# Third layer norm of a three-layer kernel: four PSUM places for rows, another order of statistics, roots and additions

## What is computed

```python
def layer_norm_2(x, g, b):
    xf = x.astype(jnp.float32)
    mu = jnp.mean(xf, axis=-1, keepdims=True)
    var = jnp.mean(jnp.square(xf - mu), axis=-1, keepdims=True)
    y = (xf - mu) * lax.rsqrt(var + LN_EPS)
    return (y * g.astype(jnp.float32) + b.astype(jnp.float32)).astype(x.dtype)
...
    h = layer_norm_2(DEEPNORM_ALPHA * h + gate[:, None, :] * y, ln_g[i], ln_b[i])   # last layer: h is the output
```

## Time and profile before

| what | before |
|---|---|
| median of 3 runs | 2042.57 us |
| the profiled execution | 2042.94 us |
| its span in the profile | 2041.1 us |
| TensorE busy | 1982.5 us (97%) |
| DVE busy | 1082.7 us (53%) |
| ACT busy | 830.3 us (41%) |
| POOL busy | 817.8 us (40%) |
| last matmul of the output projection ends | about 2017.2 us |
| last DVE instruction ends | about 2038.5 us |

### The profile page before, as it was taken

The page is one execution under the profiler, slowest core; times in us unless marked ns, Lnnn a source line. Parts: engine busy times, 40 slices in busy tenths (PEclk is TensorE's granted clock), DMA queues, the critical chain, the costliest instruction groups (busy, mean ns, idle before and its releaser), DMA issues.

```text
span 2041.1 us, 36967 instructions
## 1 busy us (share of the span) xinstructions
PE 1982.5 (97%) x14892; PEld 1641.6 (80%) x14892; DVE 1082.7 (53%) x2243; ACT 830.3 (41%) x1641; POOL 817.8 (40%) x610
## 2 busy tenths in 40 slices
PE   7999999999999999999999999999999999999896
PEld 6888888888887788888888788778888888888784
DVE  5566556766855665556666733734434334334626
ACT  4110110110126565566667610744554554555501
POOL 3433333333346622212122435645435435435546
PEclk9999999999999999999999999999999999999998
DMA  4332332332222301011001323221111111112243
GB/s 159 134 103 83 104 103 73 114 103 73 93 93 83 136 22 35 35 35 35 22 25 35 134 96 112 78 92 43 47 55 45 45 56 45 46 53 64 94 134 119
DMA packets 51063, 156.02 MB, mean 76 GB/s; under 512 B 5584, under 2 KB 9296, under 8 KB 50768
## 3 DMA queue, kind: packets, MB, share of 16 engines
q1 hardware_dynamic: 49888, 152.40, 22.5%
q10 hardware_dynamic: 1008, 1.27, 0.2%
HBM read 132.94 MB, written 20.71 MB: 75 GB/s over the span
## 4 chain that ended last, share of the span: by engine, by line
PE 64%; DVE 3%; POOL 2%; issue 2%; ACT 2%; DMA 1%; DVEq 0%; SPq 0%; POOLq 0%; ACTq 0%
PE psum L902 16%; PE psum L903 14%; PE psum L904 14%; PE psum L1086 8%; PE psum L1037 7%; PE psum L1053 5%; PE psum L911 1%; POOL w_lo L721 1%; ACT logits L1365 1%; DMA w_raw<-weights_in 1%; DVE logits L1782 1%; POOL rstd L744 0%; PE psum L1064 0%; POOL out_tile L884 0%; DVE u_lo L1669 0%
## 5 line engine op out<-in xcount | busy, mean ns | idle before, releaser
L902 PE MATMUL psum<-u_hi,w_hi 128*128 128x512 f32 (+1 forms) x1440 | 544.2, 378 | 2.6 <-DVE u_lo L1669 2.6
L903 PE MATMUL psum<-u_lo,w_hi 128*128 128x512 f32 (+1 forms) x1440 | 524.9, 364 | 0.0
L904 PE MATMUL psum<-u_hi,w_lo 128*128 128x512 f32 (+1 forms) x1440 | 524.7, 364 | 0.0
L719 POOL CAST w_hi<-w_raw 128x1024 fp32r<-128x1024 f32 x140 | 156.7, 1119 | 835.6 <-DMA w_raw<-weights_in 835.5
L721 POOL TENSOR_TENSOR w_lo<-w_raw,w_hi 128x1024 fp32r<-128x1024 f32 x140 | 350.2, 2501 | 11.2
L902 PEld LDWEIGHTS psum<-u_hi,w_hi 128*128 128x128 f32 x1440 | 271.8, 189 | 55.3 <-DVE u_lo L1669 4.4
L904 PEld LDWEIGHTS psum<-u_hi,w_lo 128*128 128x128 f32 x1440 | 272.0, 189 | 45.0
L903 PEld LDWEIGHTS psum<-u_lo,w_hi 128*128 128x128 f32 x1440 | 272.4, 189 | 38.4
L1365 ACT ACTIVATE logits<-logits,neg_max 128x640 f32<-128x640 f32 (+2 forms) x288 | 226.1, 785 | 70.9 <-DVE neg_max L1782 69.3
L1388 ACT ACTIVATE prob_t<-psum 128x320 f32<-128x320 f32 (+1 forms) x288 | 118.8, 413 | 245.2 <-PE psum L1053 244.9
L1374 ACT ACTIVATE logits<-logits,row_rec 128x640 f32<-128x640 f32 (+1 forms) x288 | 218.1, 771 | 0.0
(11 more groups left out here) (165 smaller groups left out, 2999.4 us busy)
## 6 DMA issues: line engine op xcount, KB each, us to landing
w_raw<-weights_in SPq DMA_DIRECT2D x140, 512.0 KB, 3.6
w_ada<-w_ada_in SPq DMA_DIRECT2D x48, 512.0 KB, 3.5
residual<-act_buf SPq DMA_DIRECT2D x4, 2048.0 KB, 7.6
tab<-bias_tab_in SPq DMA_DIRECT2D x16, 496.5 KB
res<-residual SPq DMA_DIRECT2D x26, 256.0 KB, 3.4
y_all<-staged SPq DMA_DIRECT2D x24, 256.0 KB, 4.9
act_buf<-x_t_in SPq DMA_DIRECT2D x8, 512.0 KB, 13.5
staged<-a_y SPq DMA_DIRECT2D x6, 640.0 KB, 2.9
```

What stands on the lines that cost most here:

```text
L719: pool.tensor_copy(w_hi[:, slot, :], w_raw[:, slot, :]).then_inc(w_hi_done, 1)
L902: pe.matmul(out, wh, xh, start=first, stop=False)
L903: pe.matmul(out, wh, xl, start=False, stop=False)
L904: return pe.matmul(out, wl, xh, start=False, stop=last)
```

## The change

Four things. (1) The norms' row places become 4 (banks 0 to 7), of which the third norm's tiles 5 and 6 use the third and fourth; tile 4 has the place of tile 2, tile 7 that of tile 3. So tile 4 waits for ACT's reading of tile 2, tile 7 for that of tile 3, and tiles 5 and 6 wait for none. The two earlier norms keep places n modulo 2. (2) The small per-tile buffers get four places, which moves every buffer behind them by 96 bytes. (3) DVE's order at the end becomes: statistics 4, product 3, statistics 5, scales 4, statistics 6, scales 5, product 4, statistics 7, scales 6, product 5, scales 7, product 6, product 7. (4) POOL's order becomes: root 2, addition 1, root 3, addition 2, root 4, addition 3, roots 5 and 6, addition 4, root 7, additions 5 and 6. ACT's and SyncE's order stay, and no arithmetic changes.

```diff
+LAST_SLOTS = {4: (0, 2), 5: (2, None), 6: (3, None), 7: (1, 3)}
+
+
+def row_slot(n):
+    return LAST_SLOTS.get(n - LN0[2], (n % ROW_SLOTS, None))[0]
+
+
+def slot_before(n):
+    if n - LN0[2] in LAST_SLOTS:
+        i = LAST_SLOTS[n - LN0[2]][1]
+        return None if i is None else LN0[2] + i
+    return n - ROW_SLOTS if n >= ROW_SLOTS else None
...
-    stats = sb("stats", [P, ROW_SLOTS, 12])
-    mean_var = sb("mean_var", [P, ROW_SLOTS, 2])
+    stats = sb("stats", [P, ROW_SLOTS + 2, 12])
+    mean_var = sb("mean_var", [P, ROW_SLOTS + 2, 2])
...
-    ps_rows = [bank(2 * n, 2) for n in range(ROW_SLOTS)]
+    ps_rows = [bank(2 * n, 2) for n in range(ROW_SLOTS + 2)]
...
-            s = slice(n % ROW_SLOTS, n % ROW_SLOTS + 1)
+            s, before = slice(row_slot(n), row_slot(n) + 1), slot_before(n)
             pool.wait_ge(ln_var, n + 1)
-            if n >= ROW_SLOTS:
-                pool.wait_ge(ln_norm, n - ROW_SLOTS + 1)
+            if before is not None:
+                pool.wait_ge(ln_norm, before + 1)
...
-        for t in range(1, S // P - 1):
+        for t in range(1, 4):
             root(2, t + 1)
             add_row(t)
+        root(2, 5)
+        root(2, 6)
+        add_row(4)
+        root(2, 7)
+        add_row(5)
+        add_row(6)
...
-            if n >= ROW_SLOTS:
-                pe.wait_ge(ln_norm, n - ROW_SLOTS + 1)
-            turn_tiles(ps_rows[n % ROW_SLOTS], [act_buf[:, k, t * P:(t + 1) * P] for k in range(KT)]).then_inc(ln_turned, 1)
+            if slot_before(n) is not None:
+                pe.wait_ge(ln_norm, slot_before(n) + 1)
+            turn_tiles(ps_rows[row_slot(n)], [act_buf[:, k, t * P:(t + 1) * P] for k in range(KT)]).then_inc(ln_turned, 1)
...
         normalise_last(3)
+        statistics(LN0[2] + 5)
         scales(LN0[2] + 4)
-        for i in range(4, S // P):
-            if i + 1 < S // P:
-                statistics(LN0[2] + i + 1)
-            normalise_last(i)
-            if i + 1 < S // P:
-                scales(LN0[2] + i + 1)
+        statistics(LN0[2] + 6)
+        scales(LN0[2] + 5)
+        normalise_last(4)
+        statistics(LN0[2] + 7)
+        scales(LN0[2] + 6)
+        normalise_last(5)
+        scales(LN0[2] + 7)
+        normalise_last(6)
+        normalise_last(7)
```

More of the change, by code:

```diff
@@ L321, in build @@
     corr = sb("corr", [P, GROUPS, PAD])
-    stats = sb("stats", [P, ROW_SLOTS, 12])
-    mean_var = sb("mean_var", [P, ROW_SLOTS, 2])
-    neg_mean = sb("neg_mean", [P, ROW_SLOTS])
-    rstd = sb("rstd", [P, ROW_SLOTS])
-    var_eps = sb("var_eps", [P, ROW_SLOTS])
+    stats = sb("stats", [P, ROW_SLOTS + 2, 12])
+    mean_var = sb("mean_var", [P, ROW_SLOTS + 2, 2])
+    neg_mean = sb("neg_mean", [P, ROW_SLOTS + 2])
+    rstd = sb("rstd", [P, ROW_SLOTS + 2])
+    var_eps = sb("var_eps", [P, ROW_SLOTS + 2])
     minus_half = sb("minus_half", [P, 1])
@@ L1478, in normalise_last @@
         def normalise_last(i):
-            place = (LN0[2] + i) % ROW_SLOTS
+            place = row_slot(LN0[2] + i)
             act.wait_ge(ln_scaled, KT + i + 1)
@@ L1636, in statistics @@
         def statistics(n):
-            s, rows = n % ROW_SLOTS, ps_rows[n % ROW_SLOTS]
+            s, rows = row_slot(n), ps_rows[row_slot(n)]
             dve.wait_ge(ln_turned, n + 1)
@@ L1645, in scales @@
         def scales(n):
-            s = n % ROW_SLOTS
+            s = row_slot(n)
             dve.wait_ge(ln_rstd, n + 1)
```

## The result

The changed kernel took 2073.5 us (median of 4 runs, 2070.96 to 2078.62), the kernel before 2043.2 beside it: a ratio of 1.015, interval 1.0138 to 1.0162. It is 1.5% slower, where +0.45 us was forecast.

A forecast was written before the change was run, and what follows sets the result against it. TensorE is busy 97% of 2041.1 us, so only the last 23 us count, bound by DVE and POOL excluding each other. +0.9, 0, -0.4, +0.6, -0.65 make +0.45 on 2042.57: 2043.0 us, range 2041.2 to 2045.2.

The forecast's parts named there:

- rival C: Large buffers moved by 96 bytes slow the first inputs' transfers at the start: 0 to 0.5 us, up to 2043.5; chance 0.10.
- 0.03 for slower: Chance given to a time more than 4.1 us slower, from a layout cost far over its bound or something unseen.
- The sign that the prediction gave for C: TensorE's last product would end more than 0.5 us later than before.
- Transposes in one go: End of kernel: tiles 4 to 7 transposed together from 2018.18, 0.72 us each; worth nothing by itself.
- Addition 4 later by 0.9: POOL at the end: addition 4 starts at 2026.85 against 2025.97, behind moved statistics, root 6 and product 4.
- Root 6 and product 4 at once, either order: Both come up within 0.1 us and run one after the other, both over at 2026.8 to 2026.9.
- Additions 4 and 5 unchanged: POOL at the end: step between these additions stays 1.08 + 0.38 + 2.35, still 3.8 us apart.
- The half step ahead of addition 6: First half of DVE's product 7 runs before POOL's addition 6, adding 0.6 us there; three half steps remain afterwards.
- rival B: DVE keeps POOL out through product 6 and tile 7's half steps, addition 6 comes last: +1.2 to +2.0 us; chance 0.10.
- The sum: End of kernel: +0.9, 0, -0.4, +0.6 and -0.65 give +0.45 us, bounds 0.0 to +0.6.
- Rival A: Roots were the delay at the end; moving them frees POOL to run beside products: 4.7 us earlier, 2037.9 us; chance 0.05.
- the shared resource: At the end, DVE's product and POOL's work exclude each other for whole instructions: 3.81 to 3.84 us a tile.

The follow-up runs named there:

- run 9: The whole change with mean_var, neg_mean and rstd laid ahead of the split weights, so weights and large buffers both move by 96 bytes, against the kernel before: 2042.8 us, ratio 1.0000.

## Why the prediction was wrong

**The failed step is rival C, the layout.** I had seen that every large buffer moves by 96 bytes, but asked only whether DVE minds (0.83 and 0.81 us on two neighbours) and how far the first transfers could suffer (0.5 us). From one engine's row I wrote that "engines don't mind". I had no row on TensorE, the one engine that is busy for 97% of the span, and such a row couldn't be had for its large products: in the kernel before all split weights and all streams stand at one distance modulo 256, so its trace is silent on any other. The rule that a condition which the trace doesn't show is bounded from both sides was needed here most: with 5952 large matmuls, 1 ns each is 6.0 us, more than the 4.1 that can be told from no change. An unbounded cost per matmul should have widened the range upwards and taken more than 0.03 for slower. The term was set at 0 to 0.5 us and measured 28 to 30. The sign that the prediction gave for C came: TensorE's last large product ended at 2045.39 + 0.40 = 2045.79 us, 28.6 later than before, where 0.5 was the bound. What the extra time is made of wasn't foreseen in any of the rivals, for C priced DVE and the transfers: here it is 6.6 ns more from one large matmul to the next.

The Trainium skill (SBUF — State Buffer, section Who interferes with whom) gives TensorE two SBUF read ports, one for the moving operand and one for the weight load, independent of each other, and says that "PE and ACT never wait on anyone". By that the distance between the two couldn't matter. The runs differ: 2043.2 us with both moved by 32 bytes, 2070.4 with the weights alone. The measurement decides, though it doesn't show which accesses collide.

**The rest held, point by point.** *Transposes in one go*: 64 matmuls in one row of 2.21 us (forecast 4 x 0.72), and of no worth by themselves, as said. *Addition 4 later by 0.9*: additions 3 and 4 start 4.64 us apart (2055.37 - 2050.73) instead of 3.81, 0.83 more. *Root 6 and product 4 at once, either order*: product 4 started at 2053.78, root 6 at 2053.82 and took 1.58, held up as before. *Additions 4 and 5 unchanged*: 3.80 apart, before 3.81. *The half step ahead of addition 6*: product 6 ended at 2062.59, the half step ran to 2063.19, addition 6 took 2.72 instead of 2.35, and DVE's next half, issued at 2063.22, took 2.71 and ended 0.54 behind it. POOL was let in between DVE instructions, so rival B didn't come. *The sum*: from the start of addition 3 to the end of addition 6 it takes 0.92 us more (forecast 1.1), from there to the end of the last DVE instruction 0.74 less (forecast 0.65); in all +0.2 us, forecast +0.45, and within the bounds of 0.0 to +0.6. *Rival A* fell twice: moving the roots gave nothing (ratio 1.0000 at the old distance), and taking the shared resource away gave 3.6 us with the roots where they were.

So the answer on the change itself, no measurable difference, was right once its side effect is taken out (run 9), and the number for the kernel as given was wrong by 30 us.

## What to carry to other kernels

Before timing an edit that adds or resizes a buffer, look at what moves behind it, and keep the distances between stationary and streamed operands of the large matmuls, and between their high and low parts, at a multiple of 256 bytes, which was the best of the eight remainders here; or pad so, and time the padding alone as a control. If a loss shows as longer steps of an engine that never idles, with the same count of instructions, look beyond the code that was changed: count instructions in a fixed stretch of both traces. And a tiny operation that looks slow (0.55 against 1.5 us) may only stand behind another engine's: take away what they share (here, one SBUF input to PSUM), not the operation.

## What was not expected of the hardware

In a steady row of the 128 x 512 matmuls that make up a fp32 product, one step takes 226.7 ns with weights and streams all at one remainder modulo 256 bytes, and 228.9 to 234.3 ns at the seven other remainders in steps of 32, at a granted clock of 1.00 from 100 to 560 us in each of these traces. The longer step is there while no other engine and no DMA packet is at work. Moving everything together by 32 bytes changes nothing (ratio 1.0006). A DVE product with one input from PSUM takes 1.22 us, as much as with both from SBUF and POOL idle (1.23), and isn't held up by POOL's additions.
